# Entry counts in place of block barriers, with three parts of the next phase issued ahead of TensorE's wait

## The reference

```
u    = rmsnorm(h); proj = u @ w_in              # 4 x 512 columns HGRN2, 4 x 512 Gated-DeltaNet, 8 gates
HGRN2, 4 heads:   q = silu, f = lb + (1-lb) sigmoid, k = 1-f, v; chunked decayed attention with a state
DeltaNet, 4 heads: q, k, v = silu(causal_conv4), l2-normalised; per chunk solve (I + A) X = rhs, then a state
y    = [gated_rmsnorm(o_hg, z_hg), gated_rmsnorm(o_gd, z_gd)]
out  = rmsnorm(h + y @ w_out), meta rows dropped
```

## Time and profile before

| | |
|---|---|
| median of 3 runs | 728.35 us |
| lowest, highest | 728.17, 728.95 us |
| the profiled execution's own time | 728.36 us |
| its span | 726.5 us |
| instructions | 13,501 |
| TensorE matmuls, union of busy time | 706.1 us |
| VectorE / ScalarE / GpSimd busy | 436.7 / 304.8 / 352.2 us |

### The profile page before, as it was taken

The page is one execution under the profiler, slowest core; times in us unless marked ns, Lnnn a source line. Parts: engine busy times, 40 slices in busy tenths (PEclk is TensorE's granted clock), DMA queues, the critical chain, the costliest instruction groups (busy, mean ns, idle before and its releaser), DMA issues. The chain is left out here.

```text
span 726.5 us, 13501 instructions
## 1 busy us (share of the span) xinstructions
PE 706.1 (97%) x4852; PEld 677.5 (93%) x4852; DVE 436.7 (60%) x1017; ACT 304.8 (42%) x798; POOL 352.2 (48%) x470
## 2 busy tenths in 40 slices
PE   7999999999999999999999999999999999999995
PEld 7799999999999999999999999999999998888884
DVE  6844356279882462598924634989436157776247
ACT  6644431725554315445444154445442352232333
POOL 5782332257563422376724332767242557765423
PEclk9999999999999999999999999999999999999998
DMA  8355332221214317441639141202254315211005
GB/s 263 39 64 83 30 33 58 48 29 31 38 30 64 50 42 63 21 39 18 46 46 69 42 65 27 33 9 48 51 74 145 86 41 200 78 54 52 29 23 209
DMA packets 63989, 44.93 MB, mean 62 GB/s; under 512 B 17438, under 2 KB 59044, under 8 KB 63924
## 3 DMA queue, kind: packets, MB, share of 16 engines
q1 hardware_dynamic: 63924, 44.07, 33.8%
HBM read 35.82 MB, written 7.65 MB: 60 GB/s over the span
## 5 line engine op out<-in xcount | busy, mean ns | idle before, releaser
L254 PE MATMUL proj<-uTh,w_high 128*128 128x352 f32 (+4 forms) x768 | 261.3, 340 | 2.4 <-PEq L1735 2.4
L254 PE MATMUL proj<-uTh,w_low 128*128 128x352 f32 (+4 forms) x768 | 245.7, 320 | 0.0
L254 PE MATMUL proj<-uTl,w_high 128*128 128x352 f32 (+4 forms) x768 | 245.2, 319 | 0.0
L254 PEld LDWEIGHTS proj<-uTh,w_high 128*128 128x128 f32 x768 | 145.1, 189 | 3.3 <-issue 3.1
L254 PEld LDWEIGHTS proj<-uTl,w_high 128*128 128x128 f32 x768 | 145.1, 189 | 0.0
L254 PEld LDWEIGHTS proj<-uTh,w_low 128*128 128x128 f32 x768 | 144.2, 188 | 0.0
L272 POOL TENSOR_TENSOR w_low<-w_raw,w_high 128x256 fp32r<-128x256 f32 (+1 forms) x54 | 71.7, 1328 | 83.2 <-ACT w_high L264 35.9
L1238 POOL TENSOR_TENSOR f_suffix<-f_suffix,f_prefix 128x192 f32<-128x192 f32 x84 | 55.6, 662 | 27.8 <-DVE f_prefix L1447 21.5
L1654 PEld LDWEIGHTS mix<-level_x 128*128 128x128 f32 x448 | 60.7, 191 | 3.5 <-issue 1.3
L1654 PE MATMUL mix<-level_x 128*128 128x64 f32 x448 | 59.7, 265 | 0.0
L1494 DVE SCALAR_TENSOR_TENSOR conv_out<-conv_in,hg_taps,conv_out 128x352 f32<-128x352 f32 (+2 forms) x81 | 51.7, 639 | 0.5
(11 more groups left out here) (305 smaller groups left out, 1394.6 us busy)
## 6 DMA issues: line engine op xcount, KB each, us to landing
w_raw<-in_w_in SPq DMA_DIRECT2D x32, 512.0 KB, 8.2
x_tile<-in_x SPq DMA_DIRECT2D x8, 512.0 KB, 6.7
w_raw<-y_scratch SPq DMA_DIRECT2D x8, 384.0 KB, 4.3
decay<-gamma_scratch SPq DMA_DIRECT2D x4, 576.0 KB, 3.8
landing<-in_w_out SPq DMA_DIRECT2D x4, 512.0 KB, 7.7
landing<-in_x SPq DMA_DIRECT2D x3, 512.0 KB, 6.3
out_y<-landing SPq DMA_DIRECT2D x3, 512.0 KB, 2.6
y_scratch<-gd_y SPq DMA_DIRECT2D x6, 192.0 KB, 1.8
```

Source lines behind the costliest of these rows:

```text
L254: last = pe.matmul(acc[:, 0:tw], w[j % 2][:, k, :], u[:, k, t0:t0 + tw], start=(k == 0 and i == 0), stop=(k == KT - 1 and i == 2))
```

## The change

All phases now lie in one block, and there is no barrier between them. A semaphore `border` counts entries: at the end of its list of a phase each of GpSimd, ScalarE, VectorE and the sync engine drains and adds one (`leave`), TensorE adds one with its first matmul of the next phase's projection, and every engine begins a phase with a wait for five times the number of the phase (`meet`). The sync engine then clears the old half of the semaphores (`clear_old`).

TensorE issues `LEAD` = 3 parts of the next phase's projection (nine matmuls) behind its last part and ahead of that wait (`lead_in`, in front of the last phase `out_lead_in`). They wait only for the weights' low half and for piece 10 to be out of its bank. All ranges of parts therefore start at 3 and not at 0. Where the three parts are taken from: in `phase_gd` from ("end",), which is what is left of 96 and falls from 5 to 2; in `phase_hg` from the last three state steps, which have 3 parts each and no longer 4, while ("end",) keeps ten. In `phase_gd` GpSimd's low halves of pieces that end in a step's last three parts are made behind the expansion of M. In the last phase one low half moves a step earlier, and VectorE takes the output pieces of the last state steps one step sooner.

```diff
+    whole = ExitStack()
+    block = whole.enter_context(nc.Block())
+    border = ctx.enter_context(nc.semaphore("border", num=SEM_LO + 2 * SEM_HALF))
+    ENGINES, LEAD = 5, 3
+    old = []
+
+    def meet(eng):
+
+        if phase[0]:
+            eng.wait_ge(border, ENGINES * phase[0])
+
+    def leave(eng):
+
+        eng.drain().then_inc(border, 1)
+
+    def clear_old(sp):
+
+        if old:
+            sp.sem_clear(range(min(old), max(old) + 1))
+
     def end_block():
...
-        nums = [s.num for s in sems.values()]
-        nc.sync.sem_clear(range(min(nums), max(nums) + 1))
+        old[:] = [s.num for s in sems.values()]
...
+                if met is not None and n == 0 and k == 0 and i == 0:
+                    last.then_inc(met, 1)
         if part == PARTS - 1:
             last.then_inc(piece_done, 1)
 
+    def lead_in(pe, kind, low):
+
+        pe.wait_ge(w_low, low)
+        pe.wait_ge(piece_out, 4 * len(PIECES) - 1)
+        for n in range(LEAD):
+            project_part(pe, n, kind, met=border)
...
+    def out_lead_in(pe, low):
+
+        pe.wait_ge(w_low, low)
+        pe.wait_ge(piece_out, 4 * len(PIECES) - 1)
+        for n in range(LEAD):
+            out_products(pe, n, met=border)
...
-        parts, at = {}, 0
+        parts, at = {}, LEAD
         for key in steps:
-            n = {"lead": 4, "end": 10}.get(key[0], 4 if key[:2] == ("rec", NG - 1) else 2)
+            n = {"lead": 4, "end": 13 - LEAD}.get(key[0], 3 if key[:2] == ("rec", NG - 1) else 2)
...
-                for n, (g, i) in enumerate(((0, 1), (0, 4), (1, 1), (1, 5), (2, 0), (2, 5))):
+            for n, (g, i) in enumerate(((0, 1), (0, 4), (1, 1), (1, 5), (2, 0), (2, 4))):
...
-                        if 2 <= n < len(steps) + 2:
-                            for idx in ends(parts[steps[n - 2]]):
+                    for lag in (2, 1):
+                        if lag <= n < len(steps) + lag and (lag == 1) == (steps[n - lag][:2] == ("rec", NG - 1)):
+                            for idx in ends(parts[steps[n - lag]]):
                                 take_out(dve, idx)
...
-        names, parts, at = [], {}, 0
+        names, parts, at = [], {}, LEAD
...
-        with nc.Block() as block:
...
+            meet(pool)
...
-                    take_low(pool, parts[key])
+                take_low(pool, parts[key][:-LEAD])
                     if key == ("blocks", 1):
                         pool.wait_ge(m_in, 16)
                         for g in range(NG):
                             expand(pool, M, blk_m, g).then_inc(m_set, 1)
+                take_low(pool, parts[key][-LEAD:])
...
+            leave(pool)
...
+            if more:
+                lead_in(pe, "hg", 4)
+            else:
+                out_lead_in(pe, 4)
...
```

More of the change, by code:

```diff
@@ new lines, in fin_low, with out_part @@
+        def fin_low(pool, which):
+            for f in which:
+                n, t, cnt = FIN[f]
+                pool.wait_ge(y_high, f + 1)
+                pool.tensor_tensor(last_ys(wl, n, t, cnt), last_from(n, t, cnt),
+                                   last_ys(wh, n, t, cnt).bitcast(F32), ALU.subtract).then_inc(y_low, 1)
+        def out_part(pe, n):
+            idx, k = divmod(n, OUT_K)
+            t, half = divmod(idx, 2)
+            if k == 0:
+                if idx >= 2:
+                    pe.wait_ge(piece_out, idx - 1)
+                if t and not half:
+                    pe.wait_ge(w_low, t)
+            last = out_products(pe, n)
+            if k == OUT_K - 1:
+                last.then_inc(piece_done, 1)
@@ new lines, in phase_gd, with take_hg @@
+        dec_in, dec_sub, dec_exp = sem("dec_in"), sem("dec_sub"), sem("dec_exp")
+        if not more:
+            wo_in, wo_late, wo_high = sem("wo_in"), sem("wo_late"), sem("wo_high")
+        def take_hg(act, rng):
+            for idx in pieces(rng):
+                take_piece(act, kind, idx)
+                if not more and idx == Y_FREE - 1:
+                    y_split_high(act, 4, Y_FREE)
+                elif idx in (2, 5) or more and idx == 8:
+                    split_high(act, idx // 3 + 2)
@@ new lines, in take_low, with wo_highs, wo_lows @@
+        def take_low(pool, rng):
+            for idx in pieces(rng):
+                if idx in (2, 5) or more and idx == 8:
+                    split_low(pool, idx // 3 + 2)
+        def wo_highs(act, ks):
+            for k in ks:
+                if k == 0:
+                    act.wait_ge(wo_in, 16 * 5)
+                if k == 3:
+                    act.wait_ge(wo_late, 16)
+                wo_split_high(act, k, LAND[k], wo_high)
+        def wo_lows(eng, ks):
+            for k in ks:
+                eng.wait_ge(wo_high, k + 1)
+                wo_split_low(eng, k, LAND[k])
@@ L1912, in _ @@
+                    decay_exp(act, i - BASE, dec_sub, dec_exp)
+                take_hg(act, parts[("B1", i)])
+                if not more and i < LEVELS - 1:
+                    wo_highs(act, ((0, 1), (2, 3, 4))[i - BASE])
+                if i < LEVELS - 1:
                     for g in range(NG):
@@ L2126, in hybrid_layer @@
     phase_hg(HEADS - 1)
+    whole.close()
+    nc.sync.sem_clear(range(min(old), max(old) + 1))
     nc.all_engine_barrier()
```

2535 lines of the change are left out of this document (1287 added, 1248 removed).

## The result

The changed kernel takes 751.23 us (median of 4 runs, 750.86 to 751.55) against 728.29 us of the kernel before: 22.9 us slower, ratio 1.031 with a 95% interval of 1.0298 to 1.0323. The prediction had the direction and the place, and a size far too small: 738.5 us, with a range that ended at 743.

A forecast was written before the change was run, and what follows sets the result against it. TensorE was taken as the bound, its matmuls covering 97% of the span. 728.36 - 7.9 (borders) + 15.4 (stalls) + 0.2 (small losses) + 2.5 (clock) = 738.56, given as 738.5 us; range 733 to 743.

The forecast's parts named there:

- The border: At the eight phase borders, nine leading matmuls cover TensorE's wait, saving 7.9 us together.
- The stall in `phase_gd`: First three DeltaNet phases, level 4: ScalarE's cast waits for its load ahead of the Y copies, costing 15.4 us.
- The other moves: Level 5's table load, part 72, ("end",) of two parts and the last phase's part 12: all costed at nothing.
- free by 0.8 us: Last phase: GpSimd's low half ends at 604.44, before TensorE reaches part 12 at about 605.3.
- the bound of 1 us: Last phase, part 12's wait for its low half: at most 1 us lost.
- The clock: Falls of the granted clock: one or two, costed at 2.5 us.
- one or two falls, 2.5 us: The clock's term in the sum: one or two falls of the granted clock, adding 2.5 us.
- 1.7 us a fall: Price of a clock fall at the range's upper end: 743 us has three falls at 1.7 us.
- three falls, or dearer ones: Rival: the DeltaNet stalls with three clock falls, or dearer ones, 741 to 747 us; 9 in 100.
- The HGRN2 phases: Three parts in each of the last three state steps, and the last phase's earlier low half: free.
- the 0.7 us in hand: HGRN2 phases: one part less between last state step and transposes still leaves head 0's normalised output 0.7 us early.
- The sum: 728.36 - 7.9 + 15.4 + 0.2 + 2.5 = 738.56, given as 738.5 us, 1.4% slower.

The follow-up runs named there:

- experiment 9: Experiment 5 with the load of experiment 8 (tile 3's load ahead of the solve's block moves): 722.41 us, ratio to before 0.991.
- experiment 6: Experiment 1 with GpSimd's low half of tile 4 in the HGRN2 phases moved behind its last inverse square root: 725.72 us, ratio to before 0.9965.
- experiment 8: The changed kernel, ScalarE's order kept, with only the sync engine's load_weights(sp, 3, ...) issued ahead of the solve's block moves: 728.80 us, ratio to before 1.0000.
- experiment 4: The changed kernel's one block and entry counts with LEAD = 0, ranges of parts as before the change: 728.03 us, ratio to before 0.9989.
- experiment 1: The changed kernel with ScalarE taking piece 8 and the cast of tile 4 behind level 4's Y copies in phase_gd, heads 0 to 2: 730.30 us.
- experiment 3: The kernel before, barriers kept, with only ScalarE's cast of tile 4 put ahead of level 4's Y copies: 750.51 us, ratio to before 1.0296.
- experiment 5: Experiment 1 with ScalarE taking piece 8 behind normalise(1) again in the HGRN2 phases: 725.21 us, ratio to before 0.9946.
- experiment 7: Experiment 1 with four parts again in the last three state steps and seven in ("end",) of the HGRN2 phases of heads 0 to 2: 732.54 us.

## Why the prediction was wrong

- **The border: right in kind, 0.6 us too high.** From the last projection part of one phase to that of the next, experiment 9 takes 0.83 to 1.07 us less than before in six of the eight. The first takes 1.03 us less in experiments 6 and 8 (in 9 a wait for gd_n stands in it), and the last 0.47 us less, since a wait of 0.3 us for a low half stands there. Together 7.3 us for 7.9. The lead covers the border in all of them, and experiment 4 shows that without it only 0.9 us of the time (1.4 us by the phases) are to be had.
- **The stall in `phase_gd`: right, in place, cause and size.** 15.2 us measured for 15.4, the three stalls at 4.35, 5.38 and 5.97 for 4.25, 5.37 and 5.78. Experiments 1, 3 and 8 each take away or add one half of the cause (the order; the load's time) and move the time by over 20 us.
- **The other moves: right in `phase_gd`, wrong by 0.3 us in the last phase.** No wait at level 5 behind the table load, none of part 72, none for ("end",) of two parts. In the last phase TensorE comes to part 12 where the prediction had it, 10.5 us into the phase, but the low half that was "free by 0.8 us" ends 1.2 us later against the start of the phase than before (at 629.04), and part 12 waits 0.3 us. That is within the bound of 1 us.
- **The clock: the step that failed by size.** I took "one or two falls, 2.5 us". No run shows that term: there were three, of 2.9 us each, 8.8 us. The 1.7 us a fall in the range is half of a row of 3.5 us in the front, 9.00 to 12.50 in the earlier trace rows, the only work at half pace in the profile of before: 17 matmuls there (15 of them of 128 columns), 33 of 128 columns in the 3.5 us behind it. Low clock there was read from the pace of the matmuls alone: the granted clock of both windows of the earlier trace rows reads 1.00 (the trace's record of the clock begins only at 12.5). The row need not show all of the stretch, and I still took it as the price. The window ahead of it has the same pace, 17 matmuls in 3.78 us of work:

```profile
5.00:9.00 4.00, 3.78 (x17) 3.56 (x17) 1.30 (x10) 2.27 (x5) 1.17 (x4) 1.00 0.92 335
```

  The two windows together would have given a stretch of over 7 us, near the 6.8 us of the changed kernel. That is an estimate: 16 of the 17 matmuls in the earlier window are of 16 x 16, a form that the trace has nowhere behind 12.5 to compare with. As for the number, the end of the kernel before shows one fall: its last matmul ends at 718.6, the granted clock is 1.00 until 722.4 and 0.50 after the earlier trace rows, a fall after 3.9 us of standing; through its borders of 0.8 us the clock stayed at 1.00. From that one row I took it that stalls can fall; every stall did, the shortest with 4.03 us of idle time. The range to 743 was drawn with 1.7 a fall. The rival "three falls, or dearer ones" had the right clock and 9 in 100; its 741 to 747 is still below the measured time, since it too had the HGRN2 phases at nothing.
- **The HGRN2 phases: the step that failed in kind.** "Free" was wrong by 6.7 us, of which 5.1 us are idle time in the two waits; around them, and once more in some heads, steps of TensorE are longer too. The rows of the third turn were read, and there the 0.7 us in hand were enough: that turn doesn't wait. What was not followed was part 71 in these phases, though it was the very part whose move made the stall in `phase_gd`: it moved from a place behind normalise(1) to one before it. Experiment 5 undoes that one move and takes back 5.1 us, which no other part of the change explains. Experiment 6 shows the second wait to be the low half's place. The parts taken from the state steps are not what makes the waits: given back, they leave the turn's whole and only cover half of the other (experiment 7).
- **The sum** with the measured terms: 728.36 - 7.3 + 15.2 + 8.8 + 6.7 = 751.8, against 751.55 for the profiled execution, whose front is 0.25 us shorter. The two failed steps weigh alike: the clock at 8.8 and not 2.5 us alone takes the sum to 744.9, the HGRN2 phases at 6.7 us alone to 745.3, both beyond the 743 at which the range ended.

**Open.** In the profiled executions the expanded blocks of head 0 came early enough in some kernels (experiments 6, 7, 8) and 0.6 to 1.0 us late in others (1, 5, 9), though 1, 5, 6 and 7 have the same DeltaNet code. Why the solve's moves vary so was not found; it blurs each comparison here by about a microsecond, as the time outside the span does. What sets the length of the low stretch, 3.4 us once and 6.8 in five cases, is open too.

## What to carry to other kernels

When a range of work shifts by n, list everything that ends in the shifted n, in every kind of phase, and look on each engine at what it is now in front of; here one part, number 71, made both losses in two kinds of phase, and only one was looked at. A wait for a transfer is only free as long as nothing urgent is queued behind it: issue the load sooner, or put the wait behind the urgent copies; either was worth over 20 us. A stall of some 4 us on a TensorE that is otherwise full is to be priced with the slow stretch that follows it, which here cost 1.5 us in one fall and 2.4 to 3.0 us in five.

## What the runs showed of the hardware

- A tap of VectorE that began inside GpSimd's 1,024-column low half was held up until 0.37 us behind the low half's end: in `phase_hg(0)` of the changed kernel one took 2.52 us and in experiment 5 one took 1.11, where the median tap takes 0.57. In the kernel before the same hold is there and small: a tap that begins at 221.40, 2.14 us into the low half, takes 0.65 us. These taps read two tiles in SBUF, `conv_in` and `conv_out`. One that had begun before the low half (at 220.39 in experiment 5, 0.56 us) and the state's update, which reads a PSUM bank (hg_state, 0.35 us), were not held, and GpSimd's own time didn't grow with the hold (2.38 us beside the tap of 2.52, 2.41 beside that of 1.11, 2.42 beside that of 0.65).
- The granted clock fell in all six stalls (4.0 to 5.8 us of idle time) of the changed kernel and of experiment 3 and in none where TensorE had unread matmuls to do; after a fall it stayed low 6.8 us five times and 3.4 us once, most of it with TensorE at work.
- Counting entries on one semaphore costs 0.22 us less than the block's barrier (0.89 for 1.11 us at a border); TensorE's wait that is left, 0.57 us, is named as ended by ScalarE's entry.
